# Feed-forward of a decoder trunk in split float32: four block-product units in place of two, with a new order

## The chip, the cores and the metric

The kernel runs on one core of a Trainium2 chip. The metric is the device time of one execution in microseconds (us); the median of several runs is compared, lower is better.

## The reference

Four layers, each x = x + 1/2 SwiGLU1(norm(x)), x = x + mixer(norm(x)), x = x + 1/2 SwiGLU2(norm(x)), with 256 tokens of 1024 channels in float32. So there are eight feed-forwards. The mixers (attention, Mamba-2, short convolution, attention) are not touched by the change.

```python
def swiglu(x, w_gu, w_down):            # w_gu: 1024 x 5632, w_down: 2816 x 1024
    gate, up = jnp.split(x @ w_gu, 2, axis=-1)
    return (jax.nn.silu(gate) * up) @ w_down
```

## The kernel before

**Numbers.** Each float32 operand is split into a high part (rounded to the fp32r format) and a low part (the rest). A product is three passes of matmuls: high x high, low x high, high x low (`PASSES`). The stationary operand is a 128x128 piece of x, the moving one 512 columns of weights.

**Blocks.** All weights come as blocks of 128 x 2048 float32 (1 MB). SyncE (queue SP) loads a block into a staging slot (`load`), ScalarE copies the high part to `w_hi` (L645, `split` of ScalarE), VectorE subtracts to get `w_lo` (L996, `split` of VectorE), and TensorE multiplies. There are `STAGE_SLOTS` = 5 staging slots and `SPLIT_SLOTS` = 3 pairs of split buffers: ScalarE may split block n only when TensorE has finished block n - 3. TensorE waits for VectorE's `lo_done` of a block. Each engine runs its own fixed list in order; on ScalarE and VectorE step i of the loop handles what block i - 1 released (`released`) and then splits block i + 2.

**Units.** The 2816 hidden columns are cut into units of 512 (the last of 256), `UNITS = "PSPSPH"`. A unit P computes gate (G0, G1 over the two halves of the channels) and up (U0, U1) in four blocks of 24 matmuls. H is the half unit, two blocks. A unit S does the same as P as a 2x2 block matrix product in the manner of Strassen and Winograd: rows are the two halves of tokens, columns gate and up, the inner dimension the two halves of channels. It has seven products of 12 matmuls: B11, B22 and B21 on loaded weight blocks and T1 to T4 on sums of weight blocks. The sums are made by VectorE in the staging slots (`weight_sum`, L1111, 128x2048 float32), sums of x once per feed-forward (`x_sums`, L1120, L1126), and the results are put together by copies on ScalarE (`part`, L715) and five partial sums on VectorE (`part_sum`, L1089). Then Silu on ScalarE (L706, L711), the gating product on VectorE (L1080, L1085), eight transposes of the hidden values on TensorE (`hidden_transpose`, L1577), and their high and low parts (L721, L1095). Down blocks D0, D1 of a unit (24 matmuls each, L1424) add into the four result banks; they come one unit later.

**The order around the change.** `ffn_order` writes the list of blocks, 39 in all. A P unit stands between S units, and both down blocks of a unit stand within the next. `gate_banks_free` makes the first block of a unit wait until the third partial sum of an S unit before it is done. Before an S unit, VectorE makes sum T1 behind the split of B11; T3 behind the hidden low parts; T2 behind the split of T3, T4 behind that of B21. Slots for loads are given out ahead by `place` in the order in which blocks are done with.

## Time and profile before

| | us |
|---|---|
| median of 3 runs | 2102.91 (2100.06 to 2106.05) |
| profiled execution, its own time | 2101.92 |
| span of the profile | 2100.2 |
| TensorE (PE) busy | 2061.0, 98% |
| VectorE (DVE) busy | 1503.2, 72% |
| ScalarE (ACT) busy | 1116.2, 53% |

Busy time is that of the instructions of an engine. The chain of work that ended last follows each step back to what released it; shares by engine say where the time went. PE is TensorE's matmuls, PEld its weight loads, SP the load queue. A matmul's duration is longer than the distance to the next one, since they are pipelined; times of a series are read from starts.

### The profile page before, as it was taken

The numbers are of one execution on the slowest core, as the hardware profiler recorded it, in microseconds if no ns is written. First come the engines' busy times: TensorE is split into PE (matmuls) and PEld (weight loads), VectorE is DVE, ScalarE is ACT, GpSimd is POOL, SyncE is SP. The second block draws the span as 40 slices with busy tenths as digits, with TensorE's granted clock in tenths as the row PEclk, the third lists the DMA queues.
The fourth block names the chain that finished last, engine by engine and source line by source line (L and its number), as shares of the span: only waits on it lengthen the run. The fifth ranks groups of instructions, "written<-read, shape, count | busy, mean of one in ns | idle before, by whom it ended". The sixth has DMA issues, their size and how long they took to land.

```text
span 2100.2 us, 25376 instructions
## 1 busy us (share of the span) xinstructions
PE 2061.0 (98%) x10493; PEld 1741.3 (83%) x10493; DVE 1503.2 (72%) x1431; ACT 1116.2 (53%) x1180; POOL 79.9 (4%) x110
## 2 busy tenths in 40 slices
PE   7999999999999999999999999999999999999998
PEld 5888887888888789988888888988888888988886
DVE  6885556885976568868776885779758776557884
ACT  5454555554654465655545554446545554556453
POOL 1000000000000002210000000000000000000000
PEclk9999999999999999999999999999999999999999
DMA  5755533655456384454575655565464665523751
GB/s 204 241 200 166 175 101 100 221 195 185 165 176 203 120 262 121 122 198 163 179 242 161 220 188 164 171 200 201 164 229 130 219 228 170 164 81 100 240 201 70
DMA packets 216838, 369.54 MB, mean 176 GB/s; under 512 B 9900, under 2 KB 92164, under 8 KB 216212
## 3 DMA queue, kind: packets, MB, share of 16 engines
q1 hardware_dynamic: 216020, 363.65, 52.5%
q0 software_dynamic: 704, 4.28, 0.5%
q8 instruction: 83, 1.36, 0.3%
q14 instruction: 31, 0.25, 0.0%
HBM read 366.81 MB, written 1.08 MB: 175 GB/s over the span
## 4 chain that ended last, share of the span: by engine, by line
PE 87%; DVE 5%; ACT 4%; POOL 1%; issue 1%; DMA 1%; SPq 0%; POOLq 0%; DVEq 0%; ACTq 0%
PE bank L1424 59%; PE bank L1545 14%; PE bank L1430 7%; ACT w_hi L645 2%; PE bank L1577 2%; DVE w_lo L996 2%; DVE arena L1295 2%; PE bank L1717 1%; PE bank L1709 1%; PE bank L1463 1%; DMA stage<-in_ssd_w_in 1%; POOL yms L579 0%; ACT arena L893 0%; PE bank L1710 0%; PE bank L1718 0%
## 5 line engine op out<-in xcount | busy, mean ns | idle before, releaser
L996 DVE TENSOR_TENSOR w_lo<-stage,w_hi 128x2048 fp32r<-128x2048 f32 (+1 forms) x248 | 560.8, 2264 | 231.5 <-ACT w_hi L645 230.6
L645 ACT ACTIVATE w_hi<-stage 128x2048 fp32r<-128x2048 f32 (+1 forms) x248 | 468.8, 1891 | 309.5 <-PE bank L1424 204.6
L996 DVE TENSOR_TENSOR w_lo<-arena,w_hi 128x2048 fp32r<-128x2048 f32 (+1 forms) x149 | 337.7, 2267 | 146.5 <-ACT w_hi L645 146.5
L1424 PE MATMUL bank<-w_hi,xt_hi 128*128 128x512 f32 (+1 forms) x1040 | 412.4, 397 | 7.1 <-ACT par L764 4.6
L1424 PE MATMUL bank<-w_lo,xt_hi 128*128 128x512 f32 (+1 forms) x1040 | 406.8, 391 | 0.0
L645 ACT ACTIVATE w_hi<-arena 128x2048 fp32r<-128x2048 f32 (+1 forms) x149 | 282.8, 1899 | 188.7 <-PE bank L1424 132.5
L1424 PE MATMUL bank<-w_hi,xt_lo 128*128 128x512 f32 (+1 forms) x1040 | 383.1, 390 | 0.0
L1424 PE MATMUL bank<-w_hi,mt_hi 128*128 128x512 f32 x864 | 341.4, 395 | 1.3 <-DVE mt_lo L1202 1.1
L1424 PE MATMUL bank<-w_hi,mt_lo 128*128 128x512 f32 x864 | 337.3, 390 | 0.0
L1424 PE MATMUL bank<-w_lo,mt_hi 128*128 128x512 f32 x864 | 336.8, 390 | 0.0
L1424 PEld LDWEIGHTS bank<-w_hi,xt_hi 128*128 128x128 f32 x1040 | 198.0, 190 | 50.8 <-issue 10.5
L1424 PEld LDWEIGHTS bank<-w_hi,xt_lo 128*128 128x128 f32 x1040 | 197.2, 190 | 40.9
L1424 PEld LDWEIGHTS bank<-w_lo,xt_hi 128*128 128x128 f32 x1040 | 198.2, 191 | 38.9
L1430 PE MATMUL bank<-xt_hi,w_hi 128*128 128x256 f32 x704 | 206.3, 294 | 0.8 <-DVE arena L1295 0.7
L1430 PE MATMUL bank<-xt_hi,w_lo 128*128 128x256 f32 x704 | 198.1, 283 | 0.0
L1430 PE MATMUL bank<-xt_lo,w_hi 128*128 128x256 f32 x704 | 195.3, 283 | 0.0
L1424 PEld LDWEIGHTS bank<-w_hi,mt_hi 128*128 128x128 f32 x864 | 162.4, 188 | 34.2 <-issue 2.3
L1424 PEld LDWEIGHTS bank<-w_hi,mt_lo 128*128 128x128 f32 x864 | 162.3, 188 | 34.2
L1424 PEld LDWEIGHTS bank<-w_lo,mt_hi 128*128 128x128 f32 x864 | 162.5, 188 | 32.1
L1430 PEld LDWEIGHTS bank<-xt_hi,w_hi 128*128 128x128 f32 x704 | 134.6, 191 | 2.6 <-issue 0.9
L1430 PEld LDWEIGHTS bank<-xt_hi,w_lo 128*128 128x128 f32 x704 | 134.7, 191 | 0.5
L1430 PEld LDWEIGHTS bank<-xt_lo,w_hi 128*128 128x128 f32 x704 | 133.0, 191 | 0.0
(191 smaller groups left out, 2345.9 us busy)
## 6 DMA issues: line engine op xcount, KB each, us to landing
stage<-in_ffn_w_gu SPq DMA_DIRECT2D x97, 1024.0 KB, 5.2
arena<-in_ffn_w_gu SPq DMA_DIRECT2D x63, 1024.0 KB, 5.2
stage<-in_ffn_w_down SPq DMA_DIRECT2D x92, 512.0 KB, 4.3
arena<-in_ffn_w_down SPq DMA_DIRECT2D x84, 512.0 KB, 4.3
stage<-in_ffn_w_gu SPq DMA_DIRECT2D x24, 512.0 KB, 4.7
arena<-in_sb_w_qkv SPq DMA_DIRECT2D x16, 512.0 KB, 4.2
stage<-in_sb_w_qkv SPq DMA_DIRECT2D x16, 512.0 KB, 4.4
stage<-in_ssd_w_in SPq DMA_DIRECT2D x8, 1024.0 KB, 5.1
```

Of the source, the lines that this page charges most:

```text
L645: act.activation(w_hi[q][:, 0:c], stage[s][:, 0:c], ACT.Copy).then_inc(hi_done, 1)
L996: dve.tensor_tensor(w_lo[q][:, 0:c], stage[s][:, 0:c], w_hi[q][:, 0:c].bitcast(F32), ALU.subtract).then_inc(lo_done, 1)
L1295: dve.scalar_tensor_tensor(chan[:, c, i:SEQ], bank[c][:, 0:SEQ - i], par[:, t:t + 1], chan[:, c, i:SEQ], ALU.mult, ALU.add).then_inc(tap_d ...
L1424: mm = pe.matmul(out_, x_[a], w[b], start=start and (a, b) == (0, 0), stop=stop and (a, b) == (1, 0))
L1430: mm = pe.matmul(out_, w[b], x_[a], start=start and (a, b) == (0, 0), stop=stop and (a, b) == (1, 0), skip_group_check=True)
L1463: mm = pe.transpose(out_, xk, ident[:, :])
L1545: mm = pe.matmul(out_[:, :], x[a], w[b], start=start and k == 0 and (a, b) == (0, 0), stop=stop and k == 3 and (a, b) == (1, 0), skip_grou ...
L1577: mm = pe.transpose(tb[b][:, c * SEQ + h * P:c * SEQ + (h + 1) * P], hid[:, h, col:col + P], ident[:, :])
L1709: pe.matmul(z[:, 0:SEQ], kk[:, 0:P], qq, start=True, stop=True, skip_group_check=True)
L1717: pe.matmul(z[:, 0:SEQ + P], neg_lower[:, :], s, start=False, stop=True, skip_group_check=True)
```

## The change

`UNITS` becomes "PSSSSH": two of three P units become S units, so four S units follow each other. The products on sums are called A1 to A4, and sums of weights are additions in place of differences, with the signs moved into the x sums and partial sums. All four weight sums of a unit stay on VectorE (`BY_DMA = 0`): A1 behind the split of B11, A3 behind the split of A1, A2 behind that of B22, A4 behind that of B21. The down block D0 of unit u - 1 stands after A1 of unit u, D1 after the first block of unit u + 1. The hidden transposes of unit u - 1 come behind that late D1 (`TURNED_AFTER`). There is a sixth staging slot; the gating buffers `sg` and `hid` lie over the buffer of squares. Blocks per feed-forward: 45.

```diff
@@ -44,11 +44,11 @@
 BLOCK = 2048
 SPLIT_SLOTS = 3
-STAGE_SLOTS = 5
+STAGE_SLOTS = 6
 SSD_STAGE_SLOTS = 3
-UNITS = "PSPSPH"
+UNITS = "PSSSSH"
 def unit_col(u):
@@ -63,23 +63,32 @@
 def ffn_order():
-    order = []
+    order, turned, late = [], {}, []
     for u, kind in enumerate(UNITS):
         down = [(u - 1, f"D{j}") for j in range(down_parts(u - 1))] if u else []
-        if kind == "P":
-            order += [(u, "G0"), (u, "G1")] + down[:1] + [(u, "U0"), (u, "U1")] + down[1:]
-        elif kind == "H":
-            order += [(u, "H0"), (u, "H1")] + down
+        own = {"P": ("G0", "G1", "U0", "U1"), "H": ("H0", "H1"),
+               "S": ("B11", "A1", "B22", "A3", "B21", "A2", "A4")}[kind]
+        own = [(u, name) for name in own]
+        order += own[:1] + late
+        if u:
+            turned[u - 1] = len(order) - 1
+        order += own[1:2]
+        if u == len(UNITS) - 1:
+            order += own[2:] + down[:1]
+            turned[u] = len(order) - 1
+            order += down[1:] + [(u, f"D{j}") for j in range(down_parts(u))]
         else:
-            order += [(u, "B11"), (u, "T1"), (u, "B22")] + down + [(u, "T3"), (u, "B21"), (u, "T2"), (u, "T4")]
-    return order + [(len(UNITS) - 1, f"D{j}") for j in range(down_parts(len(UNITS) - 1))]
+            order += down[:1] + own[2:]
+            late = down[1:]
+    return order, turned
+FFN_ORDER, TURNED_AFTER = ffn_order()
 N_UNITS, N_SUMS = len(UNITS), UNITS.count("S")
-FFN_ORDER = ffn_order()
-HOME = {"T1": "B11", "T2": "B11", "T3": "B12", "T4": "B21"}
-LAST_USE = {"B11": "T2", "B12": "T3", "B22": "B21", "B21": "T4"}
-SUM_STEP = {"T1": 1, "T3": 2, "T2": 3, "T4": 4}
+HOME = {"A1": "B11", "A2": "B11", "A3": "B12", "A4": "B21"}
+LAST_USE = {"B11": "A2", "B12": "A3", "B22": "A3", "B21": "A4"}
+BY_DMA = 0
+SUM_STEP = {"A2": 1, "A4": 2} if BY_DMA else {"A1": 1, "A3": 2, "A2": 3, "A4": 4}
 FILLERS = (((0,), (1,)), ((), (2,)), ((), (3,)), ((), (4,)))
 LAST_FILLERS = ((5,), (6,), (7,))
@@ -231,8 +240,10 @@
                 slot_of[n], loaded[n] = place(p, i, None, dmas_of(p, i))
                 continue
             u, name = FFN_ORDER[i]
-            if name == "T1":
+            if name == "B11":
+                slot_of[n], loaded[n] = home[p, u, name] = place(p, i, name, 1)
                 home[p, u, "B12"] = place(p, i, "B12", 1)
+                continue
...
@@ -300,8 +311,7 @@
-        sg = area(2 * 512).rearrange("p (h c) -> p h c", h=2)
-        hid = area(2 * 512).rearrange("p (h c) -> p h c", h=2)
+        sg, hid = squares[:, 0:2, :], squares[:, 2:4, :]
@@ -440,7 +452,7 @@
         def hidden_at(u):
-            return 4 if u == N_UNITS - 1 else 0
+            return 4 * (u % 2)
         def sum_pair(i):
@@ -636,8 +648,13 @@
                 s, q, c = slot_of[n], n % SPLIT_SLOTS, block_columns(n)
                 p = max(r for r in range(n_phases) if base[r] <= n)
                 u, name = FFN_ORDER[n - base[p]] if PHASES[p][0] == "ffn" else (0, None)
-                if name in HOME:
-                    act.wait_ge(w_summed, 4 * sums_before(nth("ffn", p), u) + SUM_STEP[name])
+                sums = sums_before(nth("ffn", p), u)
+                if name in SUM_STEP:
+                    act.wait_ge(w_summed, len(SUM_STEP) * sums + SUM_STEP[name])
+                elif name == "A1":
+                    act.wait_ge(a1_in, 16 * (sums + 1))
+                elif name == "A3":
+                    act.wait_ge(a3_in, 16 * (sums + 1))
                 else:
                     act.wait_ge(stage_in[s], loaded[n])
                 if n >= SPLIT_SLOTS:
@@ -729,27 +746,25 @@
...
-                    if name in ("G0", "H0") and u >= 1:
-                        hidden_hi(u - 1)
-                    elif name == "G1":
+                    if name == "G1":
-                    elif name == "T1":
+                    elif name == "A1":
-                        hidden_hi(u - 1)
-                    elif name == "T2":
+                    elif name == "A2":
-                    elif name == "D0" and u == N_UNITS - 2:
-                        hidden_hi(u + 1)
+                    for v in range(N_UNITS):
+                        if TURNED_AFTER[v] == i:
+                            hidden_hi(v)
-                    elif name == "T4":
+                    elif name == "A4":
@@ -1098,23 +1113,25 @@
...
+                    elif name == "A3":
+                        dve.wait_ge(stage_in[home[p, u, "B22"][0]], home[p, u, "B22"][1])
                         to, a, b = w("B12"), w("B22"), w("B12")
-                    elif name == "T2":
+                    elif name == "A2":
                         to, a, b = w("B11"), w("B22"), w("B11")
                     else:
-                        dve.wait_ge(w_summed, 4 * sums_before(f, u) + SUM_STEP["T2"])
+                        dve.wait_ge(w_summed, done + SUM_STEP["A2"])
                         to, a, b = w("B21"), w("B21"), w("B11")
-                    dve.tensor_tensor(to, a, b, ALU.subtract).then_inc(w_summed, 1)
+                    dve.tensor_tensor(to, a, b, ALU.add).then_inc(w_summed, 1)
 
                 def x_sums():
-                    for i, (a, b, op) in enumerate(((xg[:, 1, :], xg[:, 3, :], ALU.add),
+                    for i, (a, b, op) in enumerate(((xg[:, 1, :], xg[:, 3, :], ALU.subtract),
                                                     (x_sum[:, 0, :], xg[:, 0, :], ALU.subtract),
                                                     (xg[:, 0, :], xg[:, 1, :], ALU.subtract),
-                                                    (xg[:, 2, :], x_sum[:, 1, :], ALU.subtract))):
+                                                    (xg[:, 2, :], x_sum[:, 1, :], ALU.add))):
                         if i in (1, 3):
                             dve.wait_ge(x_summed, 4 * f + i)
                         dve.tensor_tensor(x_sum[:, i, :], a, b, op).then_inc(x_summed, 1)
@@ -1128,31 +1145,27 @@
...
-                    if name in ("G0", "H0") and u >= 1:
-                        hidden_lo(u - 1)
-                    elif name == "U1":
+                    if name == "U1":
-                    elif name == "T1":
-                        hidden_lo(u - 1)
-                        weight_sum(u, "T3")
-                    elif name == "T3":
+                    elif name == "A3":
-                        part_sum(u, p57, bank[6][:, :], p5, 2)
+                        part_sum(u, p57, p5, bank[6][:, :], 2, ALU.subtract)
-                        part_sum(u, sg[:, 0, :], bank[7][:, :], p1, 1)
-                    elif name == "T2":
-                        part_sum(u, hid[:, 0, :], bank[5][:, :], p16, 3)
-                        part_sum(u, hid[:, 1, :], p57, p16, 3)
-                    elif name == "T4":
+                        part_sum(u, sg[:, 0, :], bank[7][:, :], p1, 1, ALU.add)
+                    elif name == "A2":
+                        part_sum(u, hid[:, 0, :], bank[5][:, :], p16, 3, ALU.subtract)
+                        part_sum(u, hid[:, 1, :], p57, p16, 3, ALU.subtract)
+                    elif name == "A4":
-                        part_sum(u, sg[:, 1, :], bank[6][:, :], p16, 3)
+                        part_sum(u, sg[:, 1, :], bank[6][:, :], p16, 3, ALU.add)
-                    elif name == "D0" and u == N_UNITS - 2:
-                        hidden_lo(u + 1)
+                    for v in range(N_UNITS):
+                        if TURNED_AFTER[v] == i:
+                            hidden_lo(v)
@@ -1163,12 +1176,14 @@
                         split(b0 + i + 2)
                     if i + 2 < len(FFN_ORDER):
                         u, name = FFN_ORDER[i + 2]
-                        if name == "B11":
-                            weight_sum(u, "T1")
-                        elif name == "T3":
-                            weight_sum(u, "T2")
+                        if name == "B11" and not BY_DMA:
+                            weight_sum(u, "A1")
+                        elif name == "A1" and not BY_DMA:
+                            weight_sum(u, "A3")
+                        elif name == "B22":
+                            weight_sum(u, "A2")
                         elif name == "B21":
-                            weight_sum(u, "T4")
+                            weight_sum(u, "A4")
                     if i == 2 and N_SUMS:
                         x_sums_lo()
 
@@ -1597,28 +1612,27 @@
...
+                    for v in range(N_UNITS):
+                        if TURNED_AFTER[v] == i:
+                            hidden_transpose(v)
 
             def out_part(p, kq, nb, h, ks=range(4)):
 
```

**VectorE from the end of an S unit to the next unit.** Before (unit 1 into the P unit 2), from the partial sum of B21: L1089 are partial sums, L996 splits, L1085 gatings, L1095 low parts of the hidden values.

```order
L1089 TENSOR_TENSOR arena<-bank7,arena 128x512 [waits part_copied,block_used]
L996 TENSOR_TENSOR w_lo1<-arena,w_hi1 128x2048 [waits hi_done]
L1089 TENSOR_TENSOR arena<-bank5,arena 128x512 [waits part_copied]
L1089 TENSOR_TENSOR arena<-arena 128x512 [waits part_copied]
L996 TENSOR_TENSOR w_lo2<-stage0,w_hi2 128x2048 [waits hi_done]
L1089 TENSOR_TENSOR arena<-bank6,arena 128x512 [waits part_copied,block_used]
L1085 TENSOR_TENSOR arena<-arena 128x512 [waits part_summed,silu_done] x2
L996 TENSOR_TENSOR w_lo0<-stage1,w_hi0 128x2048 [waits hi_done]
```

Now (unit 1 into the S unit 2), from the same partial sum: L1104 partial sums, L1011 splits, L1128 weight sums, L1100 gatings.

```order
L1104 TENSOR_TENSOR arena<-bank7,arena 128x512 [waits part_copied,block_used]
L1011 TENSOR_TENSOR w_lo0<-stage1,w_hi0 128x2048 [waits hi_done]
L1128 TENSOR_TENSOR stage1<-arena,stage1 128x2048 [waits stage_in5]
L1104 TENSOR_TENSOR arena<-bank5,arena 128x512 [waits part_copied]
L1104 TENSOR_TENSOR arena<-arena 128x512 [waits part_copied]
L1011 TENSOR_TENSOR w_lo1<-stage0,w_hi1 128x2048 [waits hi_done]
L1104 TENSOR_TENSOR arena<-bank6,arena 128x512 [waits part_copied,block_used]
L1100 TENSOR_TENSOR arena<-arena 128x512 [waits part_summed,silu_done] x2
L1011 TENSOR_TENSOR w_lo2<-stage1,w_hi2 128x2048 [waits hi_done]
```

A weight sum (A1) now stands between the split of the next unit's first block and the third partial sum, and another (A3) before the split of the down block.

**VectorE in the middle of unit 2.** Before, unit 2 is P: splits, and with them one weight sum for unit 3 and two gatings (L1080).

```order
L996 TENSOR_TENSOR w_lo0<-stage1,w_hi0 128x2048 [waits hi_done]
L1095 TENSOR_TENSOR mt_lo<-bank6,mt_hi 128x512 [waits ht_hi_done]
L1095 TENSOR_TENSOR mt_lo<-bank7,mt_hi 128x512 [waits ht_hi_done]
L996 TENSOR_TENSOR w_lo1<-arena,w_hi1 128x2048 [waits hi_done]
L996 TENSOR_TENSOR w_lo2<-stage2,w_hi2 128x2048 [waits hi_done]
L996 TENSOR_TENSOR w_lo0<-arena,w_hi0 128x2048 [waits hi_done]
L996 TENSOR_TENSOR w_lo1<-stage0,w_hi1 128x2048 [waits hi_done]
L1111 TENSOR_TENSOR stage0<-stage1,stage0 128x2048 [waits stage_in1]
L1080 TENSOR_TENSOR arena<-bank6,arena 128x512 [waits block_used,silu_done]
L1080 TENSOR_TENSOR arena<-bank7,arena 128x512 [waits block_used,silu_done]
```

Now, unit 2 is S: low hidden parts (L1110) behind the sum A3 and the split of D0, then splits and sums in turn.

```order
L1011 TENSOR_TENSOR w_lo2<-stage1,w_hi2 128x2048 [waits hi_done]
L1128 TENSOR_TENSOR arena<-arena 128x2048 [waits stage_in3]
L1011 TENSOR_TENSOR w_lo0<-arena,w_hi0 128x2048 [waits hi_done]
L1110 TENSOR_TENSOR mt_lo<-bank6,mt_hi 128x512 [waits ht_hi_done]
L1110 TENSOR_TENSOR mt_lo<-bank7,mt_hi 128x512 [waits ht_hi_done]
L1011 TENSOR_TENSOR w_lo1<-arena,w_hi1 128x2048 [waits hi_done]
L1128 TENSOR_TENSOR stage1<-arena,stage1 128x2048
L1011 TENSOR_TENSOR w_lo2<-arena,w_hi2 128x2048 [waits hi_done]
L1011 TENSOR_TENSOR w_lo0<-stage2,w_hi0 128x2048 [waits hi_done]
L1128 TENSOR_TENSOR stage2<-stage2,stage1 128x2048 [waits w_summed]
L1011 TENSOR_TENSOR w_lo1<-stage1,w_hi1 128x2048 [waits hi_done]
L1104 TENSOR_TENSOR arena<-arena,bank6 128x512 [waits part_copied,block_used]
```

Two splits in a row with nothing between have become pairs of a sum and a split.

## Rows read from the trace of the kernel before

**Rows 1.** The page: the span, busy time by engine, the chain's shares.
```profile
span 2100.2 us, 25376 instructions
PE 2061.0 (98%) x10493; PEld 1741.3 (83%) x10493; DVE 1503.2 (72%) x1431; ACT 1116.2 (53%) x1180; POOL 79.9 (4%) x110
...
PE 87%; DVE 5%; ACT 4%; POOL 1%; issue 1%; DMA 1%; SPq 0%; POOLq 0%; DVEq 0%; ACTq 0%
```

**Rows 2.** The chain in order of time, 340:560: start us, us, what.
```profile
371.55 0.87 PE bank L1577 x8
372.43 2.92 PE bank L1545 x12
375.34 10.88 PE bank L1424 x48
386.22 10.88 PE bank L1545 x48
397.10 5.62 PE bank L1424 x24
...
403.60 27.25 PE bank L1424 x120
...
553.20 0.87 PE bank L1577 x8
```

**Rows 3.** Busy time per stretch: an S unit, a P unit, one feed-forward.
```profile
core 0: us, PE busy (x) PEld busy (x) DVE busy (x) ACT busy (x) POOL busy (x), PEclk, DMA share, GB/s
365.80:397.10 31.30, 31.24 (x141) 25.29 (x139) 31.30 (x21) 20.31 (x16) 0.00 (x0) 1.00 0.57 190
397.10:430.85 33.75, 33.75 (x154) 28.04 (x154) 22.75 (x16) 14.40 (x12) 0.00 (x0) 1.00 0.59 198
365.80:547.50 181.70, 181.64 (x828) 149.90 (x827) 138.80 (x102) 96.91 (x85) 2.62 (x4) 1.00 0.57 191
```

**Rows 4.** VectorE in one S unit: start us, us, instruction, idle before.
```profile
117.86 2.28 DVE L1111 TENSOR_TENSOR stage<-arena,stage 128x2048 f32<-128x2048 f32 x1
120.06 2.28 DVE L996 TENSOR_TENSOR w_lo<-arena,w_hi 128x2048 fp32r<-128x2048 f32 x1
...
133.60 0.68 DVE L1089 TENSOR_TENSOR arena<-bank,arena 128x512 f32<-128x512 f32 x1
134.21 2.28 DVE L996 TENSOR_TENSOR w_lo<-stage,w_hi 128x2048 fp32r<-128x2048 f32 x1
...
139.81 0.68 DVE L1089 TENSOR_TENSOR arena<-arena 128x512 f32<-128x512 f32 x1
140.40 2.28 DVE L996 TENSOR_TENSOR w_lo<-stage,w_hi 128x2048 fp32r<-128x2048 f32 x1
...
144.08 0.69 DVE L1085 TENSOR_TENSOR arena<-arena 128x512 f32<-128x512 f32 x1 [0.19 <-ACT arena L711]
```

**Rows 5.** ScalarE's groups: count, busy us and mean ns, idle before.
```profile
L645 ACT ACTIVATE w_hi<-stage 128x2048 fp32r<-128x2048 f32 (+1 forms) x248 | 468.8, 1891 | 309.5 <-PE bank L1424 204.6 <-DVE stage L1111 53.3 <-PE bank L1430 26.5
L706 ACT ACTIVATE arena<-bank,rstd 128x512 f32<-128x512 f32 (+1 forms) x64 | 37.1, 631 | 88.9 <-PE bank L1424 88.9
```

**Rows 6.** The page: DMA issues, count, KB each, us to landing.
```profile
stage<-in_ffn_w_gu SPq DMA_DIRECT2D x97, 1024.0 KB, 5.2
...
stage<-in_ffn_w_down SPq DMA_DIRECT2D x92, 512.0 KB, 4.3
```

**Rows 7.** TensorE's two long gaps: instructions, and a stretch with granted clock.
```profile
30.74 0.77 PE L1424 MATMUL bank<-w_hi,xt_hi 128*128 128x512 f32 x1 [4.64 <-ACT par L764]
31.31 0.63 PE L1424 MATMUL bank<-w_lo,xt_hi 128*128 128x512 f32 x1
...
36.99 0.39 PE L1424 MATMUL bank<-w_hi,xt_hi 128*128 128x512 f32 x1
...
709.10 5.59 PE L1461 MATMUL bank<-rstd_diag,x_res 128*128 128x128 f32 x32 [3.47 <-ACT rstd_diag L673]
...
708.00:712.00 4.00, 2.90 (x13) 2.93 (x14) 0.69 (x1) 0.78 (x3) 0.52 (x1) 0.63 0.00 0
```

More of the change, by code:

```diff
@@ L400, in build_trunk @@
         x_summed = sem("x_summed")
+        a1_in = sem("a1_in")
+        a3_in = sem("a3_in")
         xs_hi_done = sem("xs_hi_done")
@@ L1085, in hidden_summed, with part_sum @@
                     dve.tensor_tensor(hid[:, h, :], hid[:, h, :], sg[:, h, :], ALU.mult).then_inc(gated, 1)
-                def part_sum(u, to, a, b, copies):
+                def part_sum(u, to, a, b, copies, op):
                     dve.wait_ge(part_copied, 3 * sums_before(f, u) + copies)
-                    dve.tensor_tensor(to, a, b, ALU.add).then_inc(part_summed, 1)
+                    dve.tensor_tensor(to, a, b, op).then_inc(part_summed, 1)
                 def hidden_lo(u):
@@ L1100, in weight_sum @@
                     w = lambda b: stage[home[p, u, b][0]][:, :]
-                    if name == "T1":
+                    done = len(SUM_STEP) * sums_before(f, u)
+                    if name == "A1":
                         dve.wait_ge(stage_in[home[p, u, "B12"][0]], home[p, u, "B12"][1])
                         to, a, b = w("B11"), w("B12"), w("B11")
-                    elif name == "T3":
+                    elif name == "A3":
+                        dve.wait_ge(stage_in[home[p, u, "B22"][0]], home[p, u, "B22"][1])
                         to, a, b = w("B12"), w("B22"), w("B12")
-                    elif name == "T2":
+                    elif name == "A2":
                         to, a, b = w("B11"), w("B22"), w("B11")
                     else:
-                        dve.wait_ge(w_summed, 4 * sums_before(f, u) + SUM_STEP["T2"])
+                        dve.wait_ge(w_summed, done + SUM_STEP["A2"])
                         to, a, b = w("B21"), w("B21"), w("B11")
-                    dve.tensor_tensor(to, a, b, ALU.subtract).then_inc(w_summed, 1)
+                    dve.tensor_tensor(to, a, b, ALU.add).then_inc(w_summed, 1)
                 def x_sums():
-                    for i, (a, b, op) in enumerate(((xg[:, 1, :], xg[:, 3, :], ALU.add),
+                    for i, (a, b, op) in enumerate(((xg[:, 1, :], xg[:, 3, :], ALU.subtract),
                                                     (x_sum[:, 0, :], xg[:, 0, :], ALU.subtract),
                                                     (xg[:, 0, :], xg[:, 1, :], ALU.subtract),
-                                                    (xg[:, 2, :], x_sum[:, 1, :], ALU.subtract))):
+                                                    (xg[:, 2, :], x_sum[:, 1, :], ALU.add))):
                         if i in (1, 3):
@@ L1165, in ffn @@
                         u, name = FFN_ORDER[i + 2]
-                        if name == "B11":
-                            weight_sum(u, "T1")
-                        elif name == "T3":
-                            weight_sum(u, "T2")
+                        if name == "B11" and not BY_DMA:
[4 more added lines that the diff above has]
+                            weight_sum(u, "A2")
                         elif name == "B21":
-                            weight_sum(u, "T4")
+                            weight_sum(u, "A4")
                     if i == 2 and N_SUMS:
@@ L1599, in ffn @@
                         product(n, bank[4], x_part(0, 0), True, True)
-                    elif name == "T1":
+                    elif name == "A1":
                         pe.wait_ge(xs_lo_done, 4 * (f + 1))
@@ L1605, in ffn @@
                         product(n, bank[5], x_sum_part(3), False, True)
-                    elif name == "T3":
+                    elif name == "A3":
                         up_banks_free(u)
@@ L1610, in ffn @@
                         product(n, bank[7], x_part(0, 1), True, True)
-                    elif name == "T2":
+                    elif name == "A2":
                         product(n, bank[4], x_sum_part(1), False, True)
-                    elif name == "T4":
+                    elif name == "A4":
                         pe.wait_ge(part_summed, 5 * sums_before(f, u) + 1)
@@ L1617, in ffn @@
                         down(u, int(name[1]), n)
-                    if name in ("G0", "H0", "T1") and u >= 1:
-                        hidden_transpose(u - 1)
-                    elif name == "D0" and u == N_UNITS - 2:
-                        hidden_transpose(u + 1)
+                    for v in range(N_UNITS):
+                        if TURNED_AFTER[v] == i:
+                            hidden_transpose(v)
             def out_part(p, kq, nb, h, ks=range(4)):
```

## The prediction

> **What bounds the kernel now.** I read the page first, then the chain of waits over two whole feed-forwards, then the busy time per stretch, then VectorE's instructions in one unit. On the page TensorE is busy 98% and heads the chain with 87%, VectorE is busy 72% [rows 1]. In the chain the pieces of a feed-forward join without a gap: 48 matmuls of 512 columns take 10.88 us, so one starts every 0.2267 us, 24 take 5.44 and 12 take 2.72; eight transposes take 0.87; between the same transposes of two successive feed-forwards lie 553.20 - 371.55 = 181.65 us [rows 2]. TensorE waits for nobody there. So what a feed-forward costs now is its count of matmuls.
>
> The stretches say how near VectorE is behind. In a block-product unit ("S", 31.3 us) VectorE is busy 31.30 of 31.30 us; in the whole unit ("P") after it 22.75 of 33.75; over the feed-forward 138.8 of 181.7 [rows 3]. An S unit is already full for VectorE, and the P unit after it is where it catches up. Inside that unit each VectorE operation on 2048 columns starts 2.20 us before the next (117.86, 120.06), each on 512 columns 0.60 (133.60 to 134.21, 139.81 to 140.40), and nearly nothing is idle [rows 4].
>
> **The change, part by part.** *Matmuls.* A P unit has 96 in its four gate/up blocks, an S unit 7 x 12 = 84. Two units change: 24 fewer, 24 x 0.2267 = 5.44 us per feed-forward, 43.5 us over eight. This all lies on the path now, and is the whole gain possible. The splits of down weights, transposes, entry and the mixers' matmuls stay.
>
> *VectorE's work.* Per feed-forward: six blocks more (45 for 39), so six low-half splits, and eight weight sums more: 14 x 2.20 = 30.8 us. Each changed unit has seven small operations in place of two: 10 x 0.60 = 6.0. Together 36.8, on 138.8: 175.6 us, where TensorE would need 181.65 - 5.44 = 176.2. On the whole of a feed-forward the two are equal, so only the distribution decides.
>
> *The distribution.* One lap of the new order (first product of a unit to that of the next): TensorE 7 x 12 + 2 x 24 = 132 matmuls, 29.9 us, and eight transposes, 0.87: 30.8 us. VectorE: 9 splits and 4 sums, 13 x 2.20 = 28.6, five partial sums, two gatings and two low halves of hidden, 9 x 0.60 = 5.4: 34.0 us. Against 30.8 it is 3.2 us too long, in three laps following each other, with no P unit between to catch up. The lead it can have is three split buffers. It also has two waits of its own in a lap. The gating of the second half waits for the Silu behind the last partial sum, 0.2 us (0.19 in the row at 144.08 [rows 4]). The split of B21 needs the buffer of D0 three blocks earlier: from D0's start 5.44 us of matmuls and a ScalarE copy of 1.92 [rows 5], 7.4 with the handovers, while VectorE has from then 0.6 for the second low half and three operations of 2.20, 7.2: 0.3 wait. A lap is 34.6 us, 3.8 over TensorE.
>
> Where TensorE then stands in a lap: before B11 of the next unit, whose bank is freed by a partial sum that VectorE makes only behind the partial sum of B21, the split of B11 and the new sum A1: 0.60 + 2.20 + 2.20 + 0.60 = 5.6, less the 2.72 of A4's matmuls that run beside it, 2.9 us. About 0.9 more is spread before A2, A4, D1 and D0. Three laps: 3 x 3.8 = 11.5.
>
> *First S unit.* After G1's last matmul ScalarE does two Silus and the copy of B11, VectorE then split B11, sum A1, four small low halves of x sums, split A1, sum A3 and the two gatings: 1.3 + 1.92 + 4 x 2.20 + 2.4 + 1.2 = 15.6 us [rows 4, 5]. TensorE has until the hidden transposes U0, U1 and B11, 5.44 + 5.44 + 2.72 = 13.6. It waits 2.0, with the handovers 2.2; the old order had the transposes one product later and the sum of B22 and B12 behind the gatings. With 0.6 before A2 and A4: 2.8. *Last unit.* No sum follows the split of H0, so its wait is 0.7, and in the last six blocks of 5.44 VectorE is behind no more.
>
> Idle TensorE per feed-forward: 2.8 + 11.5 + 0.7 = 15.0. Net +15.0 - 5.44 = **+9.6 us**. Handovers cost a little more than start to start (2.29 long against 2.20 apart [rows 4]); a dozen of these on the path are up to 1 us. I take +10.0, times eight **+80 us**.
>
> *A rule weighed.* Rows 3 show a stretch in which VectorE is full and one in which it is two thirds busy, alternating. The Trainium skill (Perfetto Trace Analysis, Optimization Strategy) says that where the most contended engine changes over time, interleaving the regimes may help. By that, putting the full stretches together is a loss; by the occupancy over the whole (same page, Identifying the Most-Contended Engine) TensorE would stay the bound and the change give its 43.5 us. Rows 3 and 4 bear out the first here.
>
> *Edits at nothing.* A sixth staging slot: loads land in 5.2 and 4.3 us for 1 MB and for each half of a down block [rows 6]; a lap loads six blocks in 34.6 us, and the tightest one (D1, freed by the split of A3 five blocks earlier) has over 15 us. If that cover were gone, a late load would show as ScalarE waiting for a DMA. Turning the sums from differences to additions changes no count. ScalarE: nine copies and some seven small ones, about 21 us of a lap. Gating buffers laid over the squares: they are used at other times. Splitting the down blocks over two units moves D1 behind the next B11; its 5.44 us help VectorE, else every lap would stall before the transposes too; this is in the lap above.
>
> *Unknown costs, from both sides.* How much of VectorE's excess its lead hides: none, or at most three splits, 6.6 us, per feed-forward. The first lap starts with VectorE already late in my working, so I take none. The handovers: 0 to 1 us per feed-forward, 0.4 taken. The clock after the new gaps: see the rivals.
>
> **The sum.** The profiled execution took 2101.9 us for a span of 2100.2; 2101.9 + 80 = 2182. The median of the runs is 1.0 higher and I leave it at **2182 us**, 3.8% slower. A measurement of this kernel tells about 0.3% (6 us) from nothing.
>
> **Rivals.**
> *The clock falls in every lap* (10%). The gap of 4.64 us before 30.74 is followed by matmuls of 0.63 us, the low level of 1.2 GHz, and after the gap of 3.47 us ending at 709.10 the granted clock is 0.63 in the next 4 us [rows 7]. My gap is 2.9 us. If it does the same, 3.4 to 6.8 us at half speed take 1.7 to 3.4 us from TensorE; between the end of the transposes and VectorE's need of them are some 1.6 us. So 0.1 to 1.8 us a lap, 24 laps, 2 to 43 us: up to 2225. [...] Against it: the gap is shorter than both that did it.
>
> *The lead hides part* (6%). If three splits' worth, 6.6 of the 15.0, is hidden, the net is 8.4 - 5.44 = +3.0, times eight +24: 2126.
>
> *Faster: the excess is all absorbed* (5%). VectorE's total of 175.6 fits under 176.2, and if its work of the S laps were done beside the P unit and the tail, the 43.5 would be gained: 2058. It decides when VectorE needs at most 30.8 us a lap, or runs 11.5 us, five operations, ahead. Rows 3 speak for it (an S unit at 100% cost TensorE nothing); the three buffers and the order below 34.0 us speak against it.
>
> *It doesn't do what it says* (1%): the order shows it does.
>
> **How the numbers follow.** Forecast 77%, clock 10%, part hidden 6%, all absorbed 5%, no such change 1%, rest 1%. The forecast's own spread is its handovers and waits, +8.5 to +11.5 per feed-forward: 2170 to 2194. The range leaves out the partly and wholly absorbed cases mostly and takes in most of the clock case: 2158 to 2220. Faster 0.06, same 0.02, slower 0.92.
>
> **What would show it.** VectorE busy over 1770 us (1503 + 8 x 36.8 = 1797), near 97% in the feed-forwards. TensorE's matmuls of 512 columns 192 fewer and 100 to 130 us more of idle; gaps of 2.9 us at the first product of units 2, 3 and 4, released by VectorE's partial sum; a lap of 34.6 us; the feed-forward 191 to 192 us between the same transposes. In the chain VectorE's share grows from 5% to some 25% or more, all in feed-forwards. It is wrong if the lap is near 30.8 us, if ScalarE or a DMA releases the gaps, or if the low clock shows within the laps.

## The result, and the profile after

The changed kernel takes 2213.9 us (median of 4 runs, 2212.6 to 2215.8) against 2104.5 us for the kernel before on the same chip: a ratio of 1.052, 95% interval 1.050 to 1.055. It is slower by 109 us where the prediction said 80; the time lies inside its range. The profiled execution took 2214.7 us.

The page of the changed kernel, the rows that answer to [rows 1]:

```profile
span 2213.0 us, 25393 instructions
PE 2064.9 (93%) x10301; PEld 1714.8 (77%) x10301; DVE 1792.6 (81%) x1623; ACT 1229.3 (56%) x1276; POOL 79.9 (4%) x110
...
PE 60%; DVE 25%; ACT 7%; issue 6%; POOL 1%; DMA 1%; SPq 0%; ACTq 0%; POOLq 0%; DVEq 0%
```

192 matmuls are gone, as intended, and yet TensorE is busy 4 us longer, in part because some of those left ran slowly. VectorE's 1792.6 us are the 1797 of the prediction, and the chain has 25% of it, where it had 5%. TensorE's waits in the changed kernel (us in total, times, longest):

```profile
PE bank L1560 <- DVE arena L1104: 64.3, 24, 2.7
PE bank L1560 <- DVE w_lo L1011: 20.5, 32, 0.6
PE bank L1592 <- DVE arena L1095: 17.9, 7, 3.5
```

The 24 waits of 2.7 us are those before B11 of units 2 to 4, released by a partial sum (L1104): predicted 2.9. The 32 are one before A2 of each S unit; before A4 there is none. The third is the first unit's, before its hidden transposes: 17.9 us over seven, five of 2.2 and two of 3.5, predicted 2.2.

Busy time per stretch, columns as in [rows 3]: a feed-forward between the same transposes, one lap (unit 3), the lap before it, and a piece of that earlier one:

```profile
384.30:578.18 193.88, 180.59 (x804) 145.60 (x805) 174.11 (x125) 111.08 (x96) 2.62 (x4) 0.99 0.53 179
456.03:490.89 34.86, 31.53 (x142) 25.29 (x141) 32.73 (x22) 20.80 (x16) 0.00 (x0) 1.00 0.54 181
419.34:456.03 36.69, 33.37 (x143) 26.47 (x141) 35.80 (x24) 20.92 (x16) 0.00 (x0) 0.95 0.49 172
446.00:449.50 3.50, 3.50 (x11) 2.83 (x12) 3.50 (x4) 1.41 (x2) 0.00 (x0) 0.69 0.00 0
```

The lap at a full clock is 34.86 us, where 34.6 was forecast. The one before it does the same work in 36.69, with a granted clock of 0.95. Its slow piece stands right behind the wait before B11, in TensorE's instructions:

```profile
445.99 0.47 PE L1560 MATMUL bank<-w_hi,xt_hi 128*128 128x512 f32 x1 [2.68 <-DVE arena L1104]
...
446.99 0.39 PE L1560 MATMUL bank<-w_lo,xt_hi 128*128 128x512 f32 x1
447.21 0.54 PE L1560 MATMUL bank<-w_hi,xt_lo 128*128 128x512 f32 x1
447.55 0.63 PE L1560 MATMUL bank<-w_hi,xt_hi 128*128 128x512 f32 x1
```

After 2.68 us of waiting, TensorE runs five matmuls of 0.4 to 0.5 us and then goes to 0.63, the low level of 1.2 GHz. Seven times the next matmul starts 0.43 us later instead of 0.23. B11 and D1 behind the wait take 10.04 us in this lap and 8.48 in the other, 1.6 of the 1.8 us between the two. The trace has such a low stretch, 3.4 us long, in 14 of the 24 laps: 13 stretches stand behind a wait before B11, two behind the first unit's wait before its transposes.

So the profiled difference, 112.8 us, comes apart, by the starts of the hidden transposes in both traces. In the kernel before, the three intervals that became laps take 31.1, 33.6 and 31.1 us, together 95.7; three laps at the full clock take 3 x 34.83 = 104.5: +8.8. The fourth interval takes 35.5 for 33.6: +2.0. Eight times 10.8 is 86 us. The 24 laps really take 35.87 on average: 24 x 1.04 = 25 us more, most of which is the clock (e11 below puts it at some 21). The rest, +2, lies in the mixers, the entry and the stretches between feed-forwards.

### The profile page after: what moved, and what is told of

Its sections match the earlier page's. It is cut to its first block, busy times and chain, and to the rows that moved or that the text cites. A ratio compares the mean times of both kernels' runs of the same rounds, so it can differ in the third digit from the quotient of the medians.

```text
span 2213.0 us, 25393 instructions
## 1 busy us (share of the span) xinstructions
PE 2064.9 (93%) x10301; PEld 1714.8 (77%) x10301; DVE 1792.6 (81%) x1623; ACT 1229.3 (56%) x1276; POOL 79.9 (4%) x110
## 4 chain that ended last, share of the span: by engine, by line
PE 60%; DVE 25%; ACT 7%; issue 6%; POOL 1%; DMA 1%; SPq 0%; ACTq 0%; POOLq 0%; DVEq 0%
PE bank L1439 38%; DVE w_lo L1011 15%; PE bank L1560 8%; PE bank L1445 7%; ACT w_hi L662 5%; DVE arena L1104 3%; DVE stage L1128 2%; PE bank L1592 2%; DVE arena L1310 1%; DVE arena L1128 1%; PE bank L1731 1%; PE bank L1723 1%; DVE mt_lo L1143 1%; PE bank L1478 1%; DMA stage<-in_ssd_w_in 1%
## 5 line engine op out<-in xcount | busy, mean ns | idle before, releaser
L1011 DVE TENSOR_TENSOR w_lo<-stage,w_hi 128x2048 fp32r<-128x2048 f32 (+1 forms) x249 | 564.9, 2269 | 134.1 <-ACT w_hi L662 133.3
L1011 DVE TENSOR_TENSOR w_lo<-arena,w_hi 128x2048 fp32r<-128x2048 f32 (+1 forms) x196 | 443.3, 2262 | 77.0 <-ACT w_hi L662 77.0
L1439 PE MATMUL bank<-w_hi,mt_hi 128*128 128x512 f32 x864 | 343.0, 397 | 1.4 <-DVE mt_lo L1217 1.1
L1439 PE MATMUL bank<-w_hi,mt_lo 128*128 128x512 f32 x864 | 337.5, 391 | 0.0
L1439 PE MATMUL bank<-w_lo,mt_hi 128*128 128x512 f32 x864 | 337.3, 390 | 0.0
L1560 PE MATMUL bank<-w_hi,mt_hi 128*128 128x512 f32 x512 | 207.0, 404 | 20.5 <-DVE w_lo L1011 20.5
L1439 PE MATMUL bank<-w_hi,xt_hi 128*128 128x512 f32 (+1 forms) x528 | 212.4, 402 | 12.1 <-ACT par L779 4.6
L1560 PE MATMUL bank<-w_hi,xt_hi 128*128 128x512 f32 x384 | 161.2, 420 | 64.3 <-DVE arena L1104 64.3
L1439 PE MATMUL bank<-w_lo,xt_hi 128*128 128x512 f32 (+1 forms) x528 | 208.3, 394 | 0.0
L1560 PE MATMUL bank<-w_hi,mt_lo 128*128 128x512 f32 x512 | 200.9, 392 | 0.0
L1560 PE MATMUL bank<-w_lo,mt_hi 128*128 128x512 f32 x512 | 200.8, 392 | 0.0
L1439 PEld LDWEIGHTS bank<-w_hi,mt_lo 128*128 128x128 f32 x864 | 162.5, 188 | 34.8
L1439 PE MATMUL bank<-w_hi,xt_lo 128*128 128x512 f32 (+1 forms) x528 | 184.4, 392 | 0.0
L1560 PE MATMUL bank<-w_hi,xt_lo 128*128 128x512 f32 x384 | 157.3, 410 | 0.0
L1560 PE MATMUL bank<-w_lo,xt_hi 128*128 128x512 f32 x384 | 156.9, 409 | 0.0
```

The costliest lines, as they stand in the source:

```text
L1011: dve.tensor_tensor(w_lo[q][:, 0:c], stage[s][:, 0:c], w_hi[q][:, 0:c].bitcast(F32), ALU.subtract).then_inc(lo_done, 1)
L1439: mm = pe.matmul(out_, x_[a], w[b], start=start and (a, b) == (0, 0), stop=stop and (a, b) == (1, 0))
L1560: mm = pe.matmul(out_[:, :], x[a], w[b], start=start and k == 0 and (a, b) == (0, 0), stop=stop and k == 3 and (a, b) == (1, 0), skip_grou ...
```

## Experiments

All edits are on the changed kernel, unless the text says otherwise; all ratios are to the kernel before.

**e1: the new sum off the wait.** Its place goes from behind the split of B11 to behind the two partial sums.

```diff
-                        if name == "B11" and not BY_DMA:
+                        if name == "B11" and u == 1:
                             weight_sum(u, "A1")
...
+                    u, name = FFN_ORDER[min(i + 1, len(FFN_ORDER) - 1)]
+                    if name == "B11" and u > 1:
+                        weight_sum(u, "A1")
                     if i + 2 <= len(FFN_ORDER):
                         split(b0 + i + 2)
```

> The sum A1 of units 2 to 4 moves behind the two partial sums that free the banks, before the split of D1; nothing is left out, VectorE's work is the same. Theory 1 (VectorE's total work sets the lap, and the low clock after the 2.9 us gap adds to it): laps stay at 34.9 us, the gap splits into about 0.7 us before B11 and 2.3 us before D1, the low-clock intervals in the laps (16 of 3.4 us in the changed kernel) go, and the time falls by up to 16 x 1.8 = 29 us, to about 2185 us. Theory 2 (the place of A1 before the bank-freeing partial sum is the cost, not the total): the 64.3 us that TensorE waits for that partial sum mostly go, to about 2150 us. Theory 3 (the clock costs nothing because TensorE has slack in a lap): 2213 us, no change.

2215.6 us, 1.054 (1.052 to 1.056). TensorE's waits:

```profile
PE bank L1442 <- DVE w_lo L1011: 46.7, 25, 1.9
...
PE bank L1563 <- DVE arena L1104: 11.3, 24, 0.5
```

The wait of 2.7 us became 0.5 (before B11) and 1.9 (before D1), one product apart; the lap at a full clock stayed 34.82. The place of the sum moves the wait and not the lap. The low clock did not go either: 15 low stretches in the laps, as in the changed kernel, and again 13 of them behind these waits, so two short waits bring it as one of 2.7 does. The time is that of the third theory, but its reason, that TensorE has slack, was not put to the test, since the clock stayed as it was.

**e2: cheaper weight sums.** All four sums get one source.

```diff
-                    dve.tensor_tensor(to, a, b, ALU.add).then_inc(w_summed, 1)
+                    dve.tensor_scalar(to, to, 1.0, None, ALU.mult).then_inc(w_summed, 1)
```

> Leaves out the second operand of all 128 weight sums: each becomes a one-source multiplication by 1 of the same 128x2048 tile in place, same waits and same place in the order. Theory 1 (VectorE's total per lap, 34.0 us, against TensorE's 30.8): if a one-source operation takes about half of 2.20 us, VectorE needs 34.0 - 4 x 1.1 = 29.6 us, TensorE becomes the bound again, laps of 31 us, low-clock intervals gone, 2060 to 2080 us. Theory 2 (the place of A1): only 1.1 us of the 2.7 us gap goes, 24 x 1.1 = 26, about 2187 us. If the one-source operation is as long as the sum: 2214 us under both.

2113.1 us, 1.005 (1.004 to 1.007), outside both forecasts. VectorE's sums now, and the hidden transposes in the chain of waits:

```profile
L1128 DVE TENSOR_SCALAR stage<-stage 128x2048 f32<-128x2048 f32 x73 | 89.1, 1221 | 0.0
```

```profile
436.13 0.87 PE bank L1592 x8
...
468.84 0.87 PE bank L1592 x8
```

A sum takes 1.22 us for 2.29, four of them 4.3 less in a lap: VectorE needs 34.0 - 4.3 = 29.7 us and TensorE 30.8. The lap should be near 31 and is 32.7, with a wait of 1.5 us before B11 left. "VectorE has too much to do" does not explain that. The chain of the changed kernel over one lap does (start us, us, what):

```profile
456.03 0.87 PE bank L1592 x8
456.90 2.77 PE bank L1560 x12
459.67 5.45 PE bank L1439 x24
...
465.21 1.93 ACT w_hi L662
...
467.16 2.29 DVE w_lo L1011
469.46 0.46 DVE arena L1128
469.92 1.66 issue
471.57 2.10 DVE w_lo L1011
...
473.78 0.68 DVE arena L1104
474.46 2.20 DVE w_lo L1011
476.66 0.60 DVE arena L1104
477.26 2.20 DVE w_lo L1011
479.46 0.91 DVE stage L1128
480.37 1.21 issue
481.58 0.69 DVE arena L1104
...
482.41 2.97 PE bank L1560 x12
485.38 5.51 PE bank L1439 x24
490.89 0.87 PE bank L1592 x8
```

It is a loop, closed from transposes to transposes. TensorE does the transposes, A1 and D0; D0's end frees the split buffer that B21 needs (0.87 + 2.77 + 5.45); ScalarE copies B21 (1.93) and VectorE splits it (2.29); then sum A4, split A2, a partial sum, split A4, a partial sum, split B11, sum A1 and a partial sum (L1128 with the "issue" behind it is one sum of 2.1; VectorE's part, with the split of B21 and the small gaps, is 15.2); then B11 and D1 (2.97 + 5.51). Together 34.86 us. It has nine VectorE operations of the lap's 22. Only two of the four sums, A4 and A1, are in it: with 1.07 less for each it is 34.83 - 2.14 = 32.7, what e2 measured.

**e5 and e6: the sums of the loop apart from the others.** e5 has one source for A1 and A4 alone, e6 for A2 and A3 alone.

```diff
+                    if name in ("A1", "A4"):
+                        dve.tensor_scalar(to, to, 1.0, None, ALU.mult).then_inc(w_summed, 1)
+                    else:
                         dve.tensor_tensor(to, a, b, ALU.add).then_inc(w_summed, 1)
```

> Leaves out the second operand of the sums A1 and A4 only (64 of 128), as one-source operations of 1.22 us in place of 2.28. Theory L (a loop sets the lap: D0's matmuls, ScalarE's copy of B21, then on VectorE split B21, sum A4, split A2, partial sum, split A4, partial sum, split B11, sum A1, partial sum, then on TensorE B11, D1, transposes, A1 and the next D0; both shortened sums are in it): laps of 34.83 - 2 x 1.06 = 32.7 us, as with all four shortened, and the low clock goes, 2110 to 2120 us. Theory 1 (VectorE's total work per lap): 34.0 - 2.1 = 31.9 us of work, half of the gain of shortening all four, about 2160 us.

> Leaves out the second operand of the sums A2 and A3 only (64 of 128), the same amount of VectorE work less as in the run with A1 and A4. Theory L (the loop through D0, the copy of B21, A4, A1, B11 and D1): both shortened sums are outside of it, laps stay at 34.8 us and 36.5 with the low clock, 2205 to 2216 us. Theory 1 (VectorE's total): the same gain as the run with A1 and A4, about 2160 us.

e5: 2129.3 us, 1.012 (1.011 to 1.013). e6: 2203.8 us, 1.047 (1.045 to 1.049). Chain of e5, then of e6:

```profile
622.07 0.87 PE bank L1595 x8
...
655.04 0.87 PE bank L1595 x8
```

```profile
611.74 0.87 PE bank L1595 x8
...
646.60 0.87 PE bank L1595 x8
```

VectorE is spared the same time in both. In e5 the lap is 32.97 and 85 us are gained; in e6 it stays 34.86 and 10 us are gained, most of them from another place: the first unit's wait before its transposes, 17.9 us in the changed kernel, is

```profile
PE bank L1595 <- DVE arena L1095: 10.4, 7, 2.4
```

The loop sets the lap. e5's lap is 0.3 over e2's since a second loop comes into play: D0's matmuls, the copy of B21, and then VectorE's own list on to the low half of the hidden values that the next D0 needs. On VectorE it is 34.0 - 2.1 = 31.9 us of work with idle times of 0.2 (for the Silu) and 0.7 (for the copy of B21) and some 0.2 at the restarts behind them: 33.0. In the changed kernel the same list is 34.0 + 1.1 = 35.1, 0.25 over the first loop. Laps of 35.07 to 35.15 us do stand in e1 and e10, four times, each behind a lap that ran at a full clock throughout; a first lap, or one behind a low stretch at its predecessor's end, takes 34.8 to 34.9. In e6, where A3, which lies in the second loop alone, is shortened, all laps without a low stretch take 34.8 to 34.9.

Of e5's gain some is the clock: e2 has no low stretch in its laps and e5 one, behind the wait before the transposes. A single wait of 1.5 to 1.6 us before B11 left the clock alone in all 48 laps. For e5: the laps at a full clock 24 x 1.87 = 45 us, the low stretches 25, the fourth intervals (35.5 to 34.5) 8, the first units' waits 7: together 85.

**e4: two sums on GpSimd.** A2 and A3 of each unit go to GpSimd, with a semaphore of their own; the slot of B22 is held until A2 is done.

```diff
+                        pool.wait_ge(w_summed, 2 * sums_before(f, u) + 1)
+                        pool.tensor_tensor(w("B12"), w("B22"), w("B12"), ALU.add).then_inc(w_pooled, 1)
+                        pool.wait_ge(lo_done, base[p] + FFN_ORDER.index((u, "A1")) + 1)
+                        pool.tensor_tensor(w("B11"), w("B22"), w("B11"), ALU.add).then_inc(w_pooled, 1)
```

> The sums A2 and A3 of every S unit move from VectorE to the nearly idle GpSimd; nothing is left out. Theory 1: VectorE needs 34.0 - 2 x 2.20 = 29.6 us a lap, below TensorE's 30.8; GpSimd needs 2 x 4 x 1.47 = 11.8 us a lap by its 1469 ns for 128x512, which fits. Then laps of 31 to 32 us, 2065 to 2090 us, faster than both kernels. Rival: the two engines hinder each other on their reads, VectorE's 128x2048 operations get longer than 2.29 us or GpSimd's longer than 7 us, and A4's sum comes late: 2110 us or more. Theory 2 (place of A1): A1 stays where it is, so the 2.7 us gap stays, about 2200 us.

2345.9 us, 1.116 (1.114 to 1.117): 132 us slower still. One of GpSimd's sums, and VectorE beside it (start us, us, instruction):

```profile
463.81 4.61 POOL L624 TENSOR_TENSOR stage<-arena,stage 128x2048 f32<-128x2048 f32 x1 [18.90 <-DVE stage L1134]
```

```profile
463.59 0.67 DVE L1115 TENSOR_TENSOR arena<-bank,arena 128x512 f32<-128x512 f32 x1
464.19 4.77 DVE L1115 TENSOR_TENSOR arena<-arena 128x512 f32<-128x512 f32 x1
468.89 2.28 DVE L1022 TENSOR_TENSOR w_lo<-arena,w_hi 128x2048 fp32r<-128x2048 f32 x1
```

VectorE's partial sum with both sources in SBUF, 0.68 us elsewhere, takes 4.77 and ends 0.5 us behind GpSimd's instruction; the one with a PSUM source beside it takes 0.67. The trace has 18 such partial sums of 4.7 to 4.8 us, and none of the 24 with a PSUM source beside a GpSimd sum is longer than 0.69. Splits beside the other sum take 5.5 us for 2.28. All such operations together are 5.6 us a unit longer, more than the 4.4 that VectorE is spared: GpSimd gives it no time back. This run therefore says nothing for or against the loop.

**e3, e7, e8: how many block-product units, and the new order alone.** e3 is the changed kernel with `UNITS = "PSPSPH"`: the old units in the new order. e7 and e8 are the kernel before with `"PSSSSH"` and `"PSPSSH"`: the new units in the old order, five slots.

> Everything of the change but the number of block-product units: UNITS is again PSPSPH, with the new order of down blocks, sums, transposes and six slots. Theory 1 (S units behind each other are the cost): 34.9 us laps vanish, what stays is the wait of the first unit's transposes for the gating (17.9 us over 7 in the changed kernel) and some 0.6 us before A2 and A4 of each S unit: 2104 + 18 + 16 x 0.6 = about 2130 us. Theory 2 (the new order itself is slow): the 2.7 us gap before each unit that follows an S unit stays, 16 of them are 43 us more, 2170 us or more.

> The kernel before with one line changed, UNITS = PSSSSH: four S units, but its own order of sums, down blocks and transposes and five slots. Nothing is left out. If S units behind each other are the cost: VectorE has 13 operations of 2.20 and 9 of 0.60 a lap, 34.0 us, against TensorE's 30.8; three such laps, less 5.44 us of matmuls, is at least +4.2 us a feed-forward, with waits +4 to +8, 2135 to 2170 us. If the new order is the cost: below 2104 us, down to 2061. If both are, it lies 30 to 60 us below the changed kernel, as the two-unit run lies 53 above the one before.

> The kernel before with UNITS = PSPSSH: three S units in its own order, one pair behind each other, H after it. Nothing is left out. TensorE saves 12 matmuls, 2.72 us a feed-forward; VectorE is 3.2 us too long in one lap and has the H unit to catch up. If no more than that is lost: -2.7 + 3.2 = +0.5 us a feed-forward, 2106 us, no change; if the lead of three buffers hides part of it, down to 2082 us; with waits as in the changed kernel's laps (4.0 us) 2112 us.

e3: 2155.0 us, 1.025 (1.023 to 1.026). e7: 2165.6 us, 1.029 (1.028 to 1.031). e8: 2123.4 us, 1.009 (1.008 to 1.011). e3 lies between its two forecasts, e7 inside its own, e8 above all of its three. The new order costs some 50 us by itself, with the old units (e3 - before = 53) and with the new (changed - e7 = 48). Four units in series cost some 60 (e7 - before = 61, changed - e3 = 59), net of the 43.5 us of matmuls that they save. The two add up. e3's waits, none of which the kernel before has, show what the order adds; some 7 us more are low stretches behind the first of them:

```profile
PE bank L1592 <- DVE arena L1095: 17.9, 7, 3.5
PE bank L1560 <- DVE w_lo L1011: 10.2, 16, 0.6
PE bank L1439 <- DVE arena L1104: 7.5, 16, 0.5
```

In e7 nearly the whole chain of a lap is VectorE, and VectorE comes back to the same operation after 35.17 us, its 34.0 with a pause of 0.8 for a copy of ScalarE, one of 0.2 for the Silu and the restarts behind them:

```profile
79.12 2.29 DVE L996 TENSOR_TENSOR w_lo<-arena,w_hi 128x2048 fp32r<-128x2048 f32 x1 [0.78 <-ACT w_hi L645]
...
114.29 2.29 DVE L996 TENSOR_TENSOR w_lo<-stage,w_hi 128x2048 fp32r<-128x2048 f32 x1 [0.78 <-ACT w_hi L645]
```

(Its shortest interval between transposes, 34.14 us, is a first one; the 24 have a mean of 35.0.) e7 has low stretches in its laps too, one or two in each feed-forward, and they cost nothing: the four intervals add up to 136.6 to 136.8 us in all eight. TensorE has slack there. e8 says that even one pair of S units in series loses: its third interval takes 34.5 us in place of 31.1, its fourth 31.7 in place of 33.6, +1.6 for the pair although 2.7 us of matmuls are saved.

**e9: D0 one product later.** D0 is what makes the loop long, so it goes behind the unit's third product.

```diff
-            order += down[:1] + own[2:]
+            order += own[2:3] + down[:1] + own[3:]
```

> D0 of the unit before goes behind B22 instead of behind A1; the same work, nothing left out. Theory L (loop): the block whose copy waits for D0's buffer is now A2 instead of B21, so split B21 and sum A4, 4.4 us, leave the loop and one product, 2.7 us, enters: 34.83 - 4.4 + 2.7 = 33.1 us, below VectorE's own 34.0 + 0.2 us, which then sets the lap: 34.2 to 34.5 us in place of 34.83 and 36.5. 24 x 0.5 = 12 us less, 2200 us; less still if the low clock goes with it (2175), as one lap in two has it now. If only VectorE's total had counted all along: no change, 2214 us.

2211.7 us, 1.051 (1.049 to 1.054). The shortest lap is 34.18, but laps of 34.2 stand only behind laps of 37.2 with a low stretch. On average the laps are 35.8. The trace has 13 low stretches in them, and a new wait before B22: it now stands directly behind A1 and adds into A1's bank, whose result ScalarE has to copy out first (`part`, L732):

```profile
PE bank L1560 <- DVE arena L1104: 48.4, 24, 2.1
PE bank L1560 <- ACT arena L732: 24.9, 32, 0.8
```

The first loop no longer sets the lap, and the second became longer. e12 below, in the same order and with no low stretch in these laps, shows it whole; the chain comes back to D0 after 35.63 us:

```profile
425.22 5.76 PE bank L1439 x24
...
431.06 1.93 ACT w_hi L662
...
458.60 2.21 DVE w_lo L1011
...
460.85 5.75 PE bank L1439 x24
```

D0's matmuls free the buffer of A2, ScalarE copies A2, and VectorE then has 19 of its 22 operations to do up to the split of the next D0, which TensorE waits for. The text before the run left this loop out. In e9 the one lap without a low stretch that follows a full-speed lap takes 35.65 too, and a pair of 37.2 and 34.2 takes twice 35.7: the low clock costs next to nothing here (the four intervals of a feed-forward take 142.1 to 142.4 us in six of eight, with one or two low stretches, and 141.9 to 142.2 in e12 with none).

**e10: five slots.** `STAGE_SLOTS = 5` in place of 6.

> The changed kernel with STAGE_SLOTS = 5 as before; nothing left out. If loads were covered (a load lands in 5 us, the tightest one has 15 us) the slot was worth nothing: 2214 us, within 8 us. If loads are near: ScalarE waits for DMAs in the laps, and the time goes over 2225 us.

2217.6 us, 1.054 (1.052 to 1.057), laps as in the changed kernel: the sixth slot is worth nothing that these intervals can tell.

**e11 and e12: the wait filled.** Ten matmuls with no use, into a bank that is free there, stand in the wait before B11 of units 2 to 4; their results are not read. e12 does it in e9's order, with eight.

```diff
+                        if u > 1:
+                            pe.wait_ge(part_summed, 5 * sums_before(f, u) - 3)
+                            for _ in range(10):
+                                pe.matmul(bank[7][:, :], x_pair(0, 0, P)[0], w_pair(n, 0, 512)[0],
+                                          start=True, stop=True, skip_group_check=True)
                         gate_banks_free(u)
```

> Ten matmuls of 512 columns into bank 7, whose result is used by nothing, stand before the wait for the banks in front of B11 of units 2 to 4: 2.27 us of work inside the 2.69 us gap. The outputs are those of the reference. If the low clock in the laps comes from that gap and costs what the laps show (mean 35.87 against 34.83 us without it): no low interval in the laps, all laps 34.8 to 34.9 us, 24 x 1.04 = 25 us less, 2189 us. If the low clock costs nothing or comes from elsewhere: 2214 us. If the added matmuls push B11 back: up to 2225 us.

> The same filling with eight matmuls (1.81 us inside a 2.1 us gap), and D0 behind B22 as in the run that had laps of 34.18 us at best and 35.78 on average. With the clock held, the laps are 34.2 to 34.5 us everywhere: 0.3 to 0.6 us a lap under the filled run, 2174 to 2182 us. That is what is left of the change when loop and clock are taken away: VectorE's own 34.0 us a lap against TensorE's 30.8. If VectorE's total were not the floor, it would be below 2165 us.

e11: 2201.4 us, 1.047 (1.046 to 1.049). e12: 2208.3 us, 1.050 (1.049 to 1.052). In e11 the wait is

```profile
PE bank L1560 <- DVE arena L1104: 7.8, 24, 0.3
```

and all 16 second and third laps take 35.05 to 35.13 us without a low stretch. The first laps, which begin behind the transposes' wait of up to 3.5 us, have five in eight. More work on TensorE, and 12 us less time: the low clock came from the waits. Half of the expected 25 us came. The added matmuls are not the reason: 35.1 is the second loop, as in the laps of e1 and e10 without them. Three laps with no low stretch take 34.85 + 2 x 35.1 = 105.0 us, so of the 25 us only 24 x 35.87 - 8 x 105.0 = 21 are the clock, and some 8 of these stay, in the five first laps of 36.4. e12 missed: its laps have no low stretch behind the filled wait and still take 35.6, the loop shown at e9, which leaves waits of 0.8 (for ScalarE's copy) and up to 1.2 us (before D0).

Not tried: a fourth pair of split buffers, and sums made by adding DMAs. No version beats the kernel before.

## Why the prediction was right, and what failed in it

- *The saving*, 192 matmuls, 43.5 us: the count is as said, and TensorE had 24 fewer per feed-forward on its path. It was all spent.
- *VectorE's work*: 174.1 us in the feed-forward against 175.6 worked out; 1792.6 against 1797 on the page. That is 90% of a feed-forward of 193.9, not the "near 97%" of the signs.
- *The lap*: 34.6 forecast, 34.83 measured. The text's path, VectorE's 34.0 and two waits, exists: it is the second loop, 35.1 in e11. Its wait of B21's split for D0's buffer was put at 0.3 and takes 0.8 with the restart. But the text missed the other loop through the three split buffers (34.8; e2, e5 and e6 tell it from VectorE's list). Its pieces stood in the text apart, as that wait and as the order of operations before B11's bank, and were not joined. That the number came out so near is in part luck: two paths happen to lie 0.25 us apart. A forecast for cheaper sums made from the total was therefore off, in e2, by 1.7 us a lap.
- *The gap before B11*: 2.9 forecast, 2.7 measured, released by the partial sum. *First unit*: 2.2, measured 2.2 in five and 3.5 in two. The 0.6 "before A2 and A4" stands before A2 alone.
- *The sum*: +10.0 per feed-forward; without the low clock 10.8, less 0.4 between the last unit's transposes and the next feed-forward's first.
- *Edits at nothing*: the sixth slot (e10). DMA and ScalarE release none of the changed kernel's gaps in the laps.
- *The step that failed* is the clock's. The prediction gave "The clock falls in every lap" 10%, since "the gap is shorter than both that did it" [rows 7], and named a low clock within the laps as a sign of being wrong. A gap of 2.7 us does it too, behind 13 of 24, and 14 of 24 laps are slower: 21 to 25 us, and this is most of the difference between 80 and 109. The rival's price failed as well, and only its upper end covered the case: it took a low stretch of 3.4 us for 1.7, less 1.6 us of slack, so 0.1. The stretches are 3.4 us long and cost 1.6 each, since B11, D1, the transposes, A1 and D0 all lie in the loop and have no slack. The Trainium skill (TensorE: Matmul & The Clock Gate, HAM oscillation) describes a loop whose wait, of some 3 to 5 us, sends the clock down in each round. The trace agrees in kind, but with shorter waits and in 14 laps of 24; e1 shows that even waits of 0.5 and 1.9 us do it (13 of 24), e2 and e5 that one of 1.5 to 1.6 did it in none of 48, and e11 that a filled wait doesn't.
- *The rule weighed* held: by the occupancy over the whole the change would have given 43.5 us; with the full stretches in series that saving is spent and the time grows by some 60 (e7, changed against e3); the order adds the rest.
- One thing was not priced apart: the new order. The text counted it within the lap, and e3 shows that it costs some 50 us without a single unit changed.

## What to carry to other kernels

Trading work of the bound engine for work of the second one pays only where the second has room in the same stretch: add up both engines for each stretch, not for the whole, and look whether full stretches alternate with light ones. Then look for every loop through a ring of buffers (who frees the buffer, who fills it, what is queued between) and add up the length of each: only operations in the longest are worth making cheaper, and the next may lie close under it. Once TensorE, which hardly waited before, waits each round, price its clock too, also where the waits are shorter than any that the old trace shows: here 1.6 us in half of the rounds. It costs that only where TensorE's slowed work lies in the loop that sets the round; in e7 and e9 it cost next to nothing.

## What was not expected of the hardware

- Two waits of 0.5 and 1.9 us, one product apart, lowered TensorE's clock as often as one of 2.7 us (13 of 24 each); one of 1.5 to 1.6 us never did (48 laps).
- A float32 operation of VectorE on 128x2048 in SBUF takes 1.22 us with one source and 2.29 with two. The Trainium skill (VectorE: DVE Perf Modes, The perf-mode tier table) has 1227 and 2293 ns for them; the trace agrees.
- VectorE's operation with two SBUF sources waits for a whole instruction of GpSimd (0.68 became 4.77 us), and one with a PSUM source does not. GpSimd's 128x2048 addition takes 4.8 to 6.6 us in the means of its groups.
